# Moving two thirds of a modulation product from TensorE to VectorE and GpSimd

## The reference, cut to what matters

```python
sh1, sc1, g1, sh2, sc2, g2 = split(silu(c) @ w_ada + b_ada, 6)   # c: (1, 2048), w_ada: (2048, 12288)
sh1c, sc1c, ... = split(silu(c_ctx) @ w_ada + b_ada, 6)          # only shift and scale 1 are used of these
h_l = rms_norm(x, norm1_w) * (1 + sc1) + sh1
h_c = rms_norm(ctx, norm1_w) * (1 + sc1c) + sh1c
x_new = x + g1 * merge(h_l, gla(h_l, h_c), diff_attention(h_l, h_c))
x_new = x_new + g2 * conv_ffn(rms_norm(x_new, norm2_w) * (1 + sc2) + sh2)
```

## Time and profile before

| | us |
|---|---|
| median of 3 runs (2788.68 to 2795.75) | 2789.38 |
| profiled execution: time | 2797.51 |
| profiled execution: span | 2795.5 |
| TensorE matmul busy | 2587.0 (93%) |
| TensorE weight load busy | 2186.5 (78%) |
| VectorE busy | 1296.6 (46%) |
| ScalarE busy | 1073.9 (38%) |
| GpSimd busy | 43.3 (2%) |
| L643, modulation products: busy, 768 instructions | 169.9 |
| DMA: mean 163 GB/s, weights' queue | 50.4% of 16 engines |

### The profile page before, as it was taken

How to read it: one execution, slowest core, us unless ns; L and a number is a source line. 1 busy time by engine, 2 the same in 40 slices (tenths; PEclk the granted TensorE clock), 3 DMA queues, 4 the chain that set the end, 5 groups by cost and what they waited for, 6 DMA issues and landing times.

```text
span 2795.5 us, 38335 instructions
## 1 busy us (share of the span) xinstructions
PE 2587.0 (93%) x16249; PEld 2186.5 (78%) x16249; DVE 1296.6 (46%) x1748; ACT 1073.9 (38%) x1447; POOL 43.3 (2%) x53
## 2 busy tenths in 40 slices
PE   5789999988889999989999899999999999899878
PEld 1446777888678877778789888989888999897656
DVE  1212313367356444565455655565655434144454
ACT  3224223343355532343344333443545434033323
POOL 2000000011000000000000000000000000000000
PEclk9899999999899999999999999999999999697589
DMA  8655664344244468756765456555465445453024
GB/s 292 211 170 181 226 209 151 106 114 122 68 123 127 128 199 268 249 159 200 240 209 172 154 190 189 165 154 167 158 201 173 139 134 174 113 166 91 1 86 156
DMA packets 255435, 456.58 MB, mean 163 GB/s; under 512 B 20947, under 2 KB 49937, under 8 KB 253984
## 3 DMA queue, kind: packets, MB, share of 16 engines
q1 hardware_dynamic: 252672, 442.47, 50.4%
q0 software_dynamic: 2016, 7.46, 0.7%
q10 hardware_dynamic: 576, 4.19, 0.4%
HBM read 451.97 MB, written 2.10 MB: 162 GB/s over the span
## 4 chain that ended last, share of the span: by engine, by line
PE 83%; DVE 6%; ACT 3%; DMA 3%; issue 2%; DVEq 1%; POOL 0%; ACTq 0%; SPq 0%; POOLq 0%
PE psum L574 67%; PE psum L643 5%; DMA sbuf<-in_w_ada 3%; PE psum L551 2%; PE psum L1138 2%; PE psum L1100 1%; PE psum L1168 1%; DVE fast L1758 1%; ACT fast L1202 1%; PE psum L833 1%; DVE fast L1778 1%; PE psum L876 1%; PE psum L653 1%; PE psum L893 0%; PE psum L1104 0%
## 5 line engine op out<-in xcount | busy, mean ns | idle before, releaser
L574 PE MATMUL psum<-fast,fast 128*128 128x256 f32 (+4 forms) x13680 | 2089.0, 314 | 70.1 <-DVE fast L1758 52.1
L574 PEld LDWEIGHTS psum<-fast,fast 128*128 128x128 f32 (+3 forms) x13680 | 1895.3, 192 | 311.6 <-issue 105.3
L1758 DVE TENSOR_TENSOR fast<-sbuf,fast 128x1024 fp32r<-128x1024 f32 (+3 forms) x655 | 781.7, 1200 | 1152.2 <-ACT fast L1202 1149.6
L1202 ACT ACTIVATE fast<-sbuf 128x1024 fp32r<-128x1024 f32 (+3 forms) x655 | 673.9, 1032 | 1169.2 <-PE psum L574 1094.8
L1202 ACT ACTIVATE sbuf<-psum 128x512 f32<-128x512 f32 (+5 forms) x234 | 114.0, 497 | 251.6 <-PE psum L643 119.3
L643 PE MATMUL psum<-sbuf 128*32 128x512 f32 x768 | 169.9, 634 | 33.4 <-DMA sbuf<-in_w_ada 33.4
L643 PEld LDWEIGHTS psum<-sbuf 128*32 128x32 f32 x768 | 23.7, 110 | 91.0 <-DMA sbuf<-in_w_ada 62.1
L551 PE MATMUL psum<-sbuf,sbuf 128*128 128x128 f32 (+2 forms) x317 | 64.4, 317 | 29.7 <-DVE sbuf L2323 11.2
L551 PEld LDWEIGHTS psum<-sbuf,sbuf 128*128 128x128 f32 (+2 forms) x317 | 42.2, 159 | 62.8 <-issue 21.3
L1778 DVE TENSOR_TENSOR fast<-sbuf,fast 128x512 fp32r<-128x512 f32 (+3 forms) x56 | 56.9, 1016 | 4.2
L1571 ACT ACTIVATE sbuf<-psum,sbuf 128x256 f32<-128x256 f32 x88 | 43.9, 559 | 12.4 <-PE psum L574 12.4
(11 more groups left out here) (223 smaller groups left out, 1061.2 us busy)
## 6 DMA issues: line engine op xcount, KB each, us to landing
sbuf<-in_w_ada SPq DMA_DIRECT2D x192, 512.0 KB, 4.7
sbuf<-in_w_up SPq DMA_DIRECT2D x176, 512.0 KB, 4.4
sbuf<-in_w_in SPq DMA_DIRECT2D x158, 512.0 KB, 3.7
sbuf<-in_w_down SPq DMA_DIRECT2D x88, 512.0 KB, 4.3
sbuf<-in_w_gate SPq DMA_DIRECT2D x64, 512.0 KB, 3.7
sbuf<-in_w_out SPq DMA_DIRECT2D x64, 512.0 KB, 4.2
sbuf<-in_w_proj_gla SPq DMA_DIRECT2D x16, 512.0 KB, 4.6
sbuf<-in_w_proj_diff SPq DMA_DIRECT2D x16, 512.0 KB, 4.9
```

Source lines behind the costliest of these rows:

```text
L574: last = mm(out, lhsT, rhs, start=first and key not in opened, stop=end, skip_group_check=True)
L1202: return A(out, in_, ACT.Copy, scale=scale)
L1758: last = tt(lo, raw, hi.bitcast(F32), ALU.subtract)
```

## The change

The first third of the modulation (ada0 to ada7) stays on TensorE. For ada8 to ada15 VectorE, and for ada16 to ada23 GpSimd, multiply each row of weights by its value of silu(c), a scalar per partition (`csil[:, k, 0:1]`), and add the sixteen rows up into a partial row of 128 x 512 in one of two buffers `rows[a % 2]`. TensorE only folds: it sums over the partitions by a product with ones. VectorE uses scalar_tensor_tensor (multiply and add in one), two per chunk; GpSimd two tensor_scalar in the ring's slot and one or two tensor_tensor, which release the slot. ScalarE's copies of the sums fall away for these parts. `paired` takes a share num/den of plain chunks per split chunk: 3/2 over gv0 to dv1 (43 steps), 1/2 over gate6 to out1 (64 steps) and 1/2 over 64 steps from uv0's fifth chunk. The sums of chunks that follow split chunk c are done by VectorE after its subtraction of c + 1; TensorE folds after chunk c (VectorE's parts) or c + 2 (GpSimd's). GpSimd's sums stand in its program between its loads.

```diff
 class Stream:   # in __init__
-        self.paired([("gv0", ...), ("gv1", ...), ("dk0", ...), ("dk1", ...), ("dv0", ...)], ada, 8, 2)
+        self.paired([(name, panel("w_in", col, 512)) for name, col in (("gv0", 1024), ("gv1", 1536), ("dk0", 4128),
+                                                                       ("dk1", 4640), ("dv0", 5152), ("dv1", 5664))],
+                    ada, range(8, 16), 3, 2, 0)
...
-                    + [("out0", panel("w_out", 0, 512))], ada, 16, 1)
+        self.paired([(f"gate{n}", panel("w_gate", 512 * n, 512)) for n in (6, 7)]
...
+                    + [(f"out{n}", panel("w_out", 512 * n, 512)) for n in range(4)], ada, range(16, 20), 1, 2, 0)
-        self.paired(ups[:KFA // 2], ada, 20, 1, 16)
+        self.paired(ups[:KFA // 2], ada, range(20, 24), 1, 2, 12)
...
+    def paired(self, jobs, ada, parts, num, den, first):
+        todo = [(a, n, c) for a in parts for n, c in enumerate(ada[a])]
         for n, (name, c) in enumerate((name, c) for name, chunks in jobs for c in chunks):
             self.add(name, [c])
+            step = n - first
+            for a, i, x in todo[:(step + 1) * num // den - step * num // den if step >= 0 else 0]:
+                self.add(f"ada{a}", [x], 2 if a < 16 else 3)
+                if a < 16:
+                    self.beside.setdefault(self.counts[0] - 2, []).append((a, i))
+                if i == len(ada[a]) - 1:
+                    self.folds[self.counts[0] + (-1 if a < 16 else 1)] = a
+                todo = todo[1:]
...
     def released(self, g):
-        return "plain_multiplied" if self.plain[g] else "weights_split", self.nth[g] + 1
+        return ("weights_split", "plain_multiplied", "modulation_summed", "gains_summed")[self.kind[g]], self.nth[g] + 1
...
-        rows = Y(13328, 512)
+        rows = [Y(13328, 512), Y(22176, 512)]
...
 # GpSimd
+            def gain_sums(first, last):
+                for a in range(first, last):
+                    for i, g in enumerate(st.job[f"ada{a}"]):
+                        pool.wait_ge(S(st.landed(g)[0]), st.landed(g)[1])
+                        if i == 0:
+                            pool.wait_ge(S("ada_folded"), a - 1)
+                        w = ring(g)
+                        for j in range(2):
+                            end = nc.gpsimd.tensor_scalar(w[:, j, :], w[:, j, :], csil[:, 2 * i + j, 0:1], None, ALU.mult)
+                        pool.drain()
+                        if i == 0:
+                            end = nc.gpsimd.tensor_tensor(rows[a % 2], w[:, 0, :], w[:, 1, :], ALU.add)
+                        else:
+                            for j in range(2):
+                                end = nc.gpsimd.tensor_tensor(rows[a % 2], rows[a % 2], w[:, j, :], ALU.add)
+                                if j == 0:
+                                    pool.drain()
+                        end.then_inc(S("gains_summed"), 1)
...
+            gain_sums(16, 18)
             pool.wait_ge(S("split_multiplied"), st.done("pg3")[1])
...
+            gain_sums(18, 19)
             pool.wait_ge(S("split_multiplied"), st.done("pd3")[1])
...
+            gain_sums(19, 24)
             pool.wait_ge(S("mem_ready"), 8)
...
 # TensorE, gemm
                     gemm_chunk(job, q, products)
-                    next(modulation, None)
+                    if st.nth[st.job[job][q]] in st.folds:
+                        ada_fold(st.folds[st.nth[st.job[job][q]]])
...
-                    mm(bank(5), C("rowall"), rows, start=True, stop=False, skip_group_check=True)
+                    mm(bank(5), C("ones"), rows[a % 2], start=True, stop=False, skip_group_check=True)
...
 # ScalarE, steps
-                    next(modulation, None)
+                    gain_spread(st.nth[g] - 1)
                     round_chunk(st.nth[g] + 2)
...
 # VectorE, steps
                     rest_chunk(st.nth[g] + 2)
-                    next(modulation, None)
+                    for a, i in st.beside.get(st.nth[g], []):
+                        modulation_sums(a, i)
+                    if 8 <= st.folds.get(st.nth[g] - 1, 0) < 16:
+                        columns_keep(st.folds[st.nth[g] - 1])
...
+            def modulation_sums(a, i):
+                g = st.job[f"ada{a}"][i]
+                dve.wait_ge(S(st.landed(g)[0]), st.landed(g)[1])
+                if i == 0:
+                    dve.wait_ge(S("ada_folded"), a - 1)
+                for j in range(2):
+                    k, w = 2 * i + j, ring(g)[:, j, :]
+                    if k == 0:
+                        end = ts(rows[a % 2], w, csil[:, k, 0:1], None, ALU.mult)
+                    else:
+                        dve.drain()
+                        end = stt(rows[a % 2], w, csil[:, k, 0:1], rows[a % 2], ALU.mult, ALU.add)
+                end.then_inc(S("modulation_summed"), 1)
```

More of the change, by code:

```diff
@@ L152, in __init__ @@
     def __init__(self):
-        self.chunks, self.job, self.plain, self.nth = [], {}, [], []
-        self.counts = [0, 0]
+        self.chunks, self.job, self.kind, self.nth = [], {}, [], []
+        self.counts = [0, 0, 0, 0]
+        self.folds, self.beside = {}, {}
         ada = {a: panel("w_ada", c, 512) for a, c in enumerate(ADA_COLS)}
@@ L181, in __init__ @@
             self.add(f"downa{n}", panel("w_down", 512 * n, 512, rows=c))
-        self.paired(ups[KFA // 2:], ada, 24, 1)
+        for name, chunks in ups[KFA // 2:]:
+            self.add(name, chunks)
         for n in range(4):
@@ L201, in __init__, with add @@
             self.add(f"o2{n}", panel("w_out_2", 512 * n, 512))
-        self.split = [g for g, plain in enumerate(self.plain) if not plain]
-    def add(self, name, chunks, plain=False):
+        self.split = [g for g, kind in enumerate(self.kind) if not kind]
+    def add(self, name, chunks, kind=0):
         for c in chunks:
@@ L207, in add @@
             self.chunks.append(c)
[L208 to L215, removed]
+            self.kind.append(kind)
+            self.nth.append(self.counts[kind])
+            self.counts[kind] += 1
+    def paired(self, jobs, ada, parts, num, den, first):
+        todo = [(a, n, c) for a in parts for n, c in enumerate(ada[a])]
         for n, (name, c) in enumerate((name, c) for name, chunks in jobs for c in chunks):
             self.add(name, [c])
-            if n >= first + 2:
-                for other, x in todo[:per]:
-                    self.add(other, [x], True)
-                todo = todo[per:]
+            step = n - first
[6 more added lines that the diff above has]
+                todo = todo[1:]
         assert not todo
@@ L546, in _ @@
             turns = [0] * 4
[L547 removed]
+            side = iter(())
             def transposed(out, in_):
@@ L664, in ada_fold @@
                 last.then_inc(S("ada_folded"), 1)
-            def modulations(first, last, per):
-                for a in range(first, last):
-                    for i in range(0, 8, per):
-                        if i == 0 and a > first:
-                            ada_fold(a - 1)
-                        for j in range(i, i + per):
-                            ada_chunk(a, j)
-                        yield
-                ada_fold(last - 1)
-                yield
             pe.wait_ge(S("c_loaded"), 48)
@@ L809, in _ @@
             for _ in side:
-                pass
-            for _ in modulation:
                 pass
@@ L1241, in rows_copy, with gain_spread @@
                     act.wait_ge(S("ada_folded"), a)
-                copy(rows, bank(4)).then_inc(S("ada_rows_copied"), 1)
-            def modulations(first, last, per):
-                for a in range(first, last):
-                    for i in range(0, 8, per):
-                        if i == per and a > max(first, 16):
-                            spread_copy(a - 1)
-                        if i == 0 and a > first:
-                            rows_copy(a - 1)
-                        yield
-                rows_copy(last - 1)
-                yield
-                if last > 16:
-                    spread_copy(last - 1)
-            def spread_copy(a):
+                copy(rows[0], bank(4)).then_inc(S("ada_rows_copied"), 1)
+            def gain_spread(s):
+                a = st.folds.get(s, 0)
+                if a < 16:
+                    return
                 act.wait_ge(S("ada_folded"), a + 1)
@@ L1740, in _ @@
             roots = 0
-            side, modulation = iter(()), iter(())
+            side = iter(())
             def variance(out, sums, n):
```

82 lines of the change are left out of this document (29 added, 53 removed).

## The result

| | before | after |
|---|---|---|
| median of the runs, us | 2789.53 | 2853.95 (2838.09 to 2859.99) |
| profiled execution, us (span) | 2797.51 (2795.5) | 2858.39 (2856.6) |

The account below looks back on a forecast made before the run. The prediction took TensorE to bound the kernel before; +30 (A, gv0 to dv1), -25 (B, from pg0) and -18 us (C, up blocks) sum to -13, so 2784.5 in the profiled execution and 2777 in the median, range 2748 to 2838.

Parts of the forecast that it names:

- What bounds the kernel: TensorE, busy nearly all the span, with no idle time worth the name in gv0 to dv1 and pg0 to pd3.
- the removal on TensorE: 128 chunks of products leave TensorE: about 39 us gained in gv0 to dv1, 36 in pg0 to pd3, 28 in up blocks.
- Step A: gv0 to dv1: VectorE's late sums close the ring's cycle at 7.67 us per step against TensorE's 5.44; 30 us lost.
- a bound of +52: gv0 to dv1: 52 us lost if TensorE's slow restarts add 0.5 us per step.
- rival 3: Waits in gv0 to dv1 halve the clock: 131 us more, 2908; chance 0.04.
- Step B: From pg0 on: GpSimd's sums make steps of 2.95 us; after all losses 25 us gained, 36 at no loss.
- step C: Four up blocks: 56.1 us each with fold and GpSimd's operations, together 224 against 242; 18 us gained, at best 28.
- the price of GpSimd's chunk: pg0 to pd3 and up blocks: two scalar products of 0.65 and two additions of 1.2, 3.7 us a chunk.
- the ring just allows it: From pg0 on: each slot takes one GpSimd and two split chunks per 8 TensorE steps, 2.7 to 3.1 us a step.
- the loads: GpSimd's waits for the ends of pg3 and pd3 and its DMA issues delay its sums: 2 us each, 4 lost.
- Rival 1: Lock shared by VectorE and GpSimd bounds pg0 to pd3 and up blocks: 2860, or 2808 at 3.2 a step; chance 0.33.
- Rival 2: VectorE's order does no harm in gv0 to dv1 and the removal there counts in full: -82, 2707; chance 0.1.

Follow-up runs that it names:

- e7: Changed kernel with all sixteen parts summed by VectorE, right behind the subtraction of the split chunk ahead, none by GpSimd; 2720.3 us, ratio 0.9759.
- e1: Changed kernel with VectorE summing the chunks behind split chunk c right after subtracting c, one step sooner; 2791.2 us, ratio 0.9994.
- e8: Changed kernel with GpSimd's instructions of the same shapes run in its own row buffer, ring slots released by landing, g1 and g2 wrong; 2791.4 us.
- e6: Changed kernel without GpSimd's two scalar products per chunk, additions only, so g1 and g2 values are wrong; 2794.0 us.
- e10: Changed kernel without GpSimd's scalar products (g1 and g2 wrong) and with its loads of x and mem_2 issued by ScalarE; 2783.9 us.
- e4: Changed kernel with GpSimd's two scalar products per chunk replaced by one tensor_tensor over both rows, scalars broadcast; 2843.8 us.
- e12: Changed kernel with the edits of e1, e4 and e9 together, all values right; 2775.3 us.
- e9: Changed kernel with GpSimd's four loads (x after pg3, mem_2 after pd3) issued by ScalarE; 2846.0 us.

## Why the prediction was wrong, step by step

**What bounds the kernel; the removal on TensorE: right.** TensorE's busy time fell by 65. In e7 it fell by 34, 32 and 31 in A, B and C, near the counted 39, 36 and 28, but A, B and C are only 26, 19 and 20 shorter, since TensorE was idle 8, 13 and 11 us longer. It was also granted less: 0.97 and 0.98 in A of e1 and e7, where the earlier trace rows have 0.99. e7's roundings waited 85 us for transfers between 960 and 1180, and 44 us in the up blocks, which fits a ring that is late at times, but no run takes it apart. The prediction has no term for waits that come even where GpSimd does nothing. They do not turn the sign.

**Step A: right, off by 7 to 10.** +37 to +42 in the kernels that leave it alone, against +30 and a bound of +52. The cycle is 7.8 to 7.9 instead of 7.67, since from issue to rounding it took 0.2 longer beside the plain chunks: over 41 steps 5 to 9 us. gq began near 585 and not 575. The granted clock in A fell to a mean of 0.91, far from the 0.5 of rival 3: by the chain above the clock was not what set the step. (For that rival the prediction put the 1.29 us of work right before 704; they are those of 696 to 700. From 700 to 704 TensorE was busy throughout, at a mean granted clock of 0.57.)

**Step B and step C: wrong, and mainly by one term.** The step that failed is the price of GpSimd's chunk, and with it the claim that the ring just allows it. I priced GpSimd's scalar product of 128x512 at 0.65 us, nearer the memset of the earlier trace rows, and closed its range at 1.2, half the two-tensor product of the earlier trace rows. Alone it takes 1.57:

```profile
1344.47 1.57 POOL L517 TENSOR_SCALAR sbuf<-sbuf,sbuf 128x512 f32<-128x512 f32 x1 [0.17 <-issue]
```

That row is of e8. In the changed kernel the 37 products that met no instruction of VectorE took 1.55 to 1.58, and the mean over all is 2.0. It is dearer than an operation on two tensors of that size (1.3 alone), so neither row bounded it. With it a chunk is 7.7 us and not 3.7, over the 5.76 of two steps, and B and C end at +21 and +6 instead of -25 and -18. That is 70 of the 74 us by which the profiled execution missed its 2784.5. At 3.2 us a chunk (e6) C is -17.5, the predicted -18; B is -4.8, and -15.7 with the loads elsewhere (e10). So of the 46 us missed in B some 26 are the chunk's price and 7 the loads (11 measured, 4 predicted). The other 13 stand in e10 too. e7, where VectorE does the sums, has -19.3, only 3.6 less, so most of the 13 is not GpSimd's own: in e7 TensorE was idle 13 us longer in B than before.

The way the prediction adds up is wrong as well. With 1.57 for the product its own sum has 2 x 1.57 + 2 x 1.2 + 2 x 1.09 = 7.7 us for two steps, as measured, but then gives B about +33 and C about +41. Measured were +21 and +6. Once GpSimd sets the pace a block lasts as long as its eight chunks (62.0 us both), and the fold and VectorE's closing operations run inside that time; the prediction put them on top.

The Trainium skill had seemed to back the 0.65: "GPSIMD Engine Reference", Engine selection, calls one-input operations roughly line rate and two-input ones about twice as slow as VectorE's. The 1.57 us for one tensor and a scalar per partition, against 1.3 for two tensors and against VectorE's 0.48 for its tensor_scalar, contradict its first half; the measurement decides.

**Rival 1: the number, not its mechanism.** 2854 lies in its 2808 to 2860, in part by luck: A cost 10 us more than it has, and C 18 less than its +24 though the steps were longer than its 3.6. It let a shared lock be the bound, on VectorE's side. e8 shows that in C the lock alone does not cost what the changed kernel lost: it makes both engines' instructions longer (subtractions of up to 2.3 us, GpSimd's product from 1.57 to a mean of 2.0), and the harm comes where GpSimd's longer chunk holds a slot and, behind it, the one queue of all weights. The Trainium skill's "SBUF — State Buffer", Who interferes with whom, calls the lock exclusive and has whoever issues first block the other for its whole instruction. GpSimd's operations on two tensors agree: the subtraction that began at 1342.94 beside the one of 1342.86 ended 1.09 us after it, like that of the earlier trace rows. The scalar product agrees only where VectorE came first: right behind a running subtraction it took 2.6. Where the product came first it did not hold VectorE to its end. The subtraction at 1345.82 above took its own 1.23, though a product had been running since 1345.04, and so did all ten in the changed kernel that began 0.77 us or more into a product of at most 1.65 us. **Rival 2** had the size of what A can give wrong, even in the better order: -21 to -26, not -39. **The range** ended at 2838 and left out the far end of rival 1; it hung on the product's price, which no row showed.

**Open.** At 5.6 us a chunk (e4, e12) GpSimd is not always busy and C is still at 0 to +1. That landing, sums and release, one after another in four slots, set the pace there would fit the 95 us for which SyncE's queue waited for GpSimd between 1305 and 1560 in e4, but no run took this apart. Nor is it shown why B has 11 us more in e8 than in e7; 3.7 of them stand in pd1 to pd3 and 6.2 in out0 to out2.

## What to carry to other kernels

An engine that reads from a shared ring has to be costed by how long it holds a slot and in which place of its program it lets go: VectorE's sums one step later cost 61 us, with the same instructions and the same busy time. An operation that the trace does not hold has a price that is open upward as well; a cheaper-looking neighbour is no upper bound, and one trial of that instruction alone would have turned the sign of this forecast. Before work goes to an idle engine, look whether the busier one does it so much faster that it is the better place.

## What the runs showed of the hardware

- GpSimd, 128x512 float32: tensor_scalar with a scalar per partition 1.57 us alone, 2.0 on average in the changed kernel; tensor_tensor 1.3 alone, 1.7 on average; one tensor_tensor of 128x1024 with the scalars broadcast (e4) 1.9 alone, 2.34 on average. VectorE makes product and sum of the same 128x512 tile in 0.75.
- VectorE's subtraction of two tensors and a two-tensor operation of GpSimd exclude each other: a subtraction that started second ended 1.08 us after the other's end, where alone it takes 1.23, and a GpSimd operation that started right behind a subtraction took 2.3 in place of 1.3. GpSimd's scalar product does so only at its start: beside products that took their own 1.57 (changed kernel, e1, e8, e9), a subtraction that began 0.1 to 0.4 us into the product took 1.4 to 1.7, and one that began 0.8 us or more into it took its own 1.23.
- A drain on GpSimd behind two transfers issued by itself lasted 5.9 to 7.3 us in the changed kernel and e8; moving the four issues to ScalarE took 9 to 11 us out of B.
